# TensorE's expert jobs written out, and the last job's rows added to the tokens by gate matrices on chip

## The chip, the cores and the metric

The kernel runs on one core of a Trainium2 chip. Its time is device time in microseconds from a run's start to its end; lower is better. In the trace, PE is TensorE's matmul side and PEld its weight loads, DVE is VectorE, ACT is ScalarE, POOL is GpSimd, and SP is the engine whose queue issues most DMAs.

## The reference

Two layers of a hybrid backbone over 256 latent tokens of width 1024 with 256 context tokens. The change lies in the channel mixer of the second layer, a top-2-of-8 expert SwiGLU in float32, and in the norm and residual behind it:

```python
logits = (xt @ w_router) + b_router
top_v, top_e = lax.top_k(logits, TOP_K)            # TOP_K = 2, N_EXPERTS = 8
gates = jax.nn.softmax(top_v, axis=-1)
...
def expert_block(args):
    xblk, e = args
    g, u = jnp.split(xblk @ w_gu[e], 2, axis=-1)   # 1024 -> 2 x 3584
    return (jax.nn.silu(g) * u) @ w_dn[e]          # 3584 -> 1024
yb = yb * row_gate[:, None]
... .at[row_tok].add(yb)                           # each token: the sum of its two gated rows
x = x + gt2 * rmsnorm(channel_mixer(hx, ...), g_post_ffn[l])
```

The kernel returns the latent stream after both layers.

## The kernel before

Everything up to the router (both mixers, the dense feed-forward network of layer 0) is untouched by the change and ends at about 1,376 us of the span. What follows is the expert stage.

**Jobs.** The 512 token-expert pairs are sorted by expert and cut into jobs of at most `CAP` = 96 rows of one expert. DVE works out on chip the list of jobs, their number, and for each token the two rows that it holds in that list (`rt[:, 0:4]`, and as whole numbers `posi`) with the two gates (`rt[:, 4:8]`). With the inputs given there are 8 jobs, one for each expert. POOL scatters the token rows to DRAM (`moe_rows`), from where SP fetches the 96 rows of a job.

**A job on PE.** A job's weights are 42 slabs of 1 MB: 28 for gate and up (seven groups `q` of four), 14 for down. SP brings them into a ring of 14 slab buffers; it issues a slab when PE has released the buffer (`e_used`), and PE waits for it by `e_raw`. Each slab is 24 float32 matmuls of 256 columns, which go to four column groups of the array (`products`, L1691; the trace shows each as two records, so 48 records a slab). After the first slab of each group PE transposes the group before (`transposes`, three, L1701), between DVE's product and copy; after the seventh down slab it transposes the next job's rows (eight, L1723). On PE, ACT and DVE the job is the body of a loop (`Fori(0, n_jobs)`) whose count is read from `jobs` at run time; SP has job 0 written out and a loop over the rest.

**Order around a job's end.** ACT takes silu of each group's gate half (L892, L894), copies the next job's rows out of PSUM (L885), then the result `O` to `yb` (L898, L899), and sends it to DRAM (`moe_out`) by four DMAs (L902), whose landings count in `y_out`. `yb` holds 96 rows in an odd form: partition 32c + r and index g are row 32g + r and columns 256c to 256c + 255.

**After the last job.** ACT waits for all landings (L905), loads a table and signals POOL, which fetches each token's two rows of `moe_out` by four indirect DMAs (L605, `back`). ACT multiplies the first by its gate (L909), DVE adds the gated second (L1344), ACT squares and sums (L912) and takes the root (L914), DVE forms a diagonal of reciprocals (L1347, L1348), PE multiplies tokens by it, which also turns them (L1732), DVE adds them to the stream `xm` (L1351), and SP writes it out (L555).

Of the kernel before, what the change touches and what calls it, by code (L numbers as in the profile page):

```python
# [28 lines left out]
P = 128  # L29
D = 1024  # L30
# [28 lines left out]
N_LIST = MAX_JOBS + 1  # L59

# [92 lines left out]
def build_program(nc, a, out):  # L153
    ctx = ExitStack()
    with ctx:
# [73 lines left out]
        back = [[view(M, 8192 + 2048 * c + D * n, D) for n in range(2)] for c in range(2)]  # L229
        part1 = [view(M, 12288 + D * n, D) for n in range(2)]  # L230
# [62 lines left out]
        f_part, f_tok, f_sq, f_sd, f_diag, f_t = (sem(n) for n in ("f_part", "f_tok", "f_sq", "f_sd", "f_diag", "f_t"))  # L293
# [185 lines left out]
        def _(sp):  # L479
# [53 lines left out]
            n_jobs = sp.value_load(jobs[0:1, N_LIST:N_LIST + 1], min_val=1, max_val=MAX_JOBS)  # L533
# [10 lines left out]
            with sp.Fori(1, n_jobs) as j:  # L544
                e = sp.value_load(jobs[0:1, bass.ds(j, 1)], min_val=0, max_val=NE - 1)
                for i in range(JOB_SLABS):
                    sp.wait_ge(e_used, j * JOB_SLABS + (i + 1))
                    expert_slab(e, i, i)
                    if i == 12:
                        sp.wait_ge(e_gath, j + 1)  # L550
                        rows_of(j + 1)

# [60 lines left out]
        def _(act):  # L613
# [265 lines left out]
            n_jobs = act.value_load(jobs[0:1, N_LIST:N_LIST + 1], min_val=1, max_val=MAX_JOBS)  # L879
# [9 lines left out]
            with act.Fori(0, n_jobs) as j:  # L889
                for q in range(GU_GROUPS):  # L890
                    act.wait_ge(e_used, j * JOB_SLABS + (RAW_E + 4 * q + 4))
                    act.activation(tge[:, q % 2, 0:2, :], S[q % 2][:, :].rearrange("p (a b) -> p a b", b=256)[:, :, 0:P],  # L892
                                   ACT.Silu).then_inc(e_silu, 1)
                    act.activation(tge[:, q % 2, 2, :], T[q % 2][:, 0:P], ACT.Silu).then_inc(e_silu, 1)  # L894
                take_rows(j + 1)
                act.wait_ge(e_used, j * JOB_SLABS + (RAW_E + JOB_SLABS))
                act.wait_ge(y_out, j * 64 + 64)
                act.activation(yb[:, 0:2, :], O[0][:, :].rearrange("p (a b) -> p a b", b=256), ACT.Copy).then_inc(e_yb, 1)  # L898
                act.activation(yb[:, 2, :], O[1][:, 0:256], ACT.Copy).then_inc(e_yb, 1)  # L899
                act.wait_ge(e_yb, j * 2 + 4)  # L900
                for c in range(4):
                    act.dma_start(ys[bass.ds(j, 1), :, :, 256 * c:256 * c + 256].rearrange("a g p n -> (a p) g n"),  # L902
                                  yb[32 * c:32 * c + 32, :, :]).then_inc(y_out, 16)

            act.wait_ge(y_out, n_jobs * 64 + 64)  # L905
            act.activation(tab[:], eps[0:1, :], ACT.Sqrt).then_inc(ys_ready, 1)
            for n in range(2):
                act.wait_ge(rows_back[0][n], 16)
                act.activation(part1[n], back[0][n], ACT.Copy, scale=rt[:, 4 + n:5 + n]).then_inc(f_part, 1)  # L909
            for n in range(2):  # L910
                act.wait_ge(f_tok, n + 1)
                act.activation(part1[n], ytok[n], ACT.Square, accum_out=rt[:, 176 + n:177 + n]).then_inc(f_sq, 1)  # L912
                act.wait_ge(f_sq, n + 1)
                act.activation(rt[:, 178 + n:179 + n], rt[:, 176 + n:177 + n], ACT.Sqrt, scale=1.0 / D, bias=eps[:]).then_inc(f_sd, 1)  # L914
# [5 lines left out]
        def _(dve):  # L920
# [390 lines left out]
            own.link(dve.tensor_copy(jobs[0:1, N_LIST:N_LIST + 1], end[0:1, 7:8]))  # L1311
            dve.wait_ge(ht_copied, 4)
            own.link(dve.memset(rt[0:1, 160:161], 0.0))
            dve.memset(rt[0:1, 163:164], 0.0).then_inc(y_out, 64)
# [3 lines left out]
            n_jobs = dve.value_load(jobs[0:1, N_LIST:N_LIST + 1], min_val=1, max_val=MAX_JOBS)  # L1318
# [6 lines left out]
            with dve.Fori(0, n_jobs) as j:  # L1325
# [23 lines left out]
            for k in range(KT):  # L1349
                dve.wait_ge(f_t, k // 2 + 1)  # L1350
                dve.scalar_tensor_tensor(xm[:, 0, k, :], [S[0], S[1], T[0], T[1]][k // 2][:, SEQ * (k % 2):SEQ * (k % 2) + SEQ],  # L1351
# [6 lines left out]
        def _(pe):  # L1358
# [19 lines left out]
            def keep_up(n):  # L1378

                for _ in range(n):  # L1380
                    mm(T[1][:, 0:P], mean[:], mean[:], start=True, stop=True)
# [292 lines left out]
            n_jobs = pe.value_load(jobs[0:1, N_LIST:N_LIST + 1], min_val=1, max_val=MAX_JOBS)  # L1674
# [9 lines left out]
            with pe.Fori(0, n_jobs) as j:  # L1684
# [20 lines left out]
                for q in range(GU_GROUPS):  # L1705
                    if q >= 2:
                        pe.wait_ge(e_h, j * 2 * GU_GROUPS + (2 * q - 2))
                    for s in range(4):
                        products(4 * q + s, lambda k, g: xg[:, 2 * s + k, 32 * g:32 * g + 32], (S[q % 2], T[q % 2]), s == 0, s == 3)
                        if s == 0 and q:  # L1710
                            transposes(q - 1)
                pe.wait_ge(e_yb, j * 2 + 2)
                for d in range(DN_SLABS):
# [5 lines left out]
                    if d == 6:  # L1719
# [6 lines left out]

            for n in range(2):
                pe.wait_ge(f_diag, n + 1)
            for k in range(KT):
                for n in range(2):  # L1730
                    c = SEQ * (k % 2) + P * n
                    ins = mm([S[0], S[1], T[0], T[1]][k // 2][:, c:c + P], ytok[n][:, P * k:P * k + P], diag[:, n, :],  # L1732
# [164 lines left out]
```

## Time and profile before

| | us |
|---|---|
| median of 3 runs | 2393.02 (2390.64 to 2393.62) |
| the profiled execution, its own time | 2392.59 |
| its span, first to last instruction | 2390.8 |
| PE busy | 2274.5 (95%) |
| DVE / ACT / POOL busy | 752.7 / 572.0 / 48.5 |
| expert stage on PE, first to last slab matmul | 1397.17 to 2363.14 |
| from there to the span's end | 27.7 |

PE's busy share hides what matters here: a pause of 5 to 6 us between two jobs is 4% of a job. The span is read in three parts: up to 1,397 us (layers before the expert jobs), the eight jobs, and the end. Only the last two are touched, save for a few small instructions of the router. A pause of PE shows in the timeline as an idle time in square brackets with what ended it; "issue" there means that no semaphore seen by the profile did. PEclk in a table of stretches is the granted clock of TensorE, 1.00 being 2.4 GHz and 0.50 being 1.2 GHz.

### The profile page before, as it was taken

How to read it: one execution, taken by the hardware profiler on the slowest of the kernel's cores; microseconds unless marked ns; L12 is line 12 of the kernel's file. 1: busy time of each engine (PE TensorE's matmuls, PEld its weight loads, DVE VectorE, ACT ScalarE, POOL GpSimd, SP SyncE). 2: the span in 40 equal slices, each digit the busy share in tenths (PEclk: the TensorE clock that was granted, in tenths of full speed). 3: DMA queues.
4: the chain of work that ended last, by engine and by line, in shares of the span. 5: the costliest groups of instructions: out<-in, count | busy, mean ns of one | idle time of the engine just before them, and what ended most of it. 6: DMA issues, size and time to landing. Idle time of an engine off the chain costs nothing.

```text
span 2390.8 us, 55761 instructions
## 1 busy us (share of the span) xinstructions
PE 2274.5 (95%) x24654; PEld 1644.5 (69%) x24654; DVE 752.7 (31%) x1513; ACT 572.0 (24%) x1094; POOL 48.5 (2%) x63
## 2 busy tenths in 40 slices
PE   7999999999999999989999999899999999999996
PEld 4777877777777887768989875555555555555554
DVE  4465345445532233477377610000101010101011
ACT  4245334323322222245355410000000000000001
POOL 0000010000200000000010000000000000000000
PEclk8999999999999999999999999999999999999998
DMA  6323232324843343212234869999999999999991
GB/s 248 116 107 141 82 130 97 133 106 159 284 176 118 127 176 131 97 65 96 105 137 146 315 265 393 361 376 356 385 365 379 362 379 362 378 358 386 361 377 63
DMA packets 86755, 549.92 MB, mean 230 GB/s; under 512 B 10336, under 2 KB 13920, under 8 KB 26496
## 3 DMA queue, kind: packets, MB, share of 16 engines
q1 hardware_dynamic: 76176, 521.91, 57.3%
q0 software_dynamic: 4176, 14.81, 1.9%
q10 hardware_dynamic: 6176, 9.70, 1.3%
q8 instruction: 200, 3.28, 0.5%
q14 instruction: 27, 0.22, 0.0%
HBM read 529.47 MB, written 16.91 MB: 229 GB/s over the span
## 4 chain that ended last, share of the span: by engine, by line
PE 44%; issue 43%; DVE 8%; ACT 2%; DMA 1%; POOL 0%; ACTq 0%; POOLq 0%; SPq 0%; DVEq 0%
PE pp L1363 9%; PE pp L1365 8%; PE pp L1364 8%; PE S L1363 2%; DVE wsp L926 2%; PE S L1364 2%; PE S L1365 2%; PE T L1365 2%; PE T L1363 2%; PE T L1364 2%; PE pp L1398 1%; PE T L1494 1%; ACT wsp L622 1%; PE O L1481 1%; PE S L1461 1%
## 5 line engine op out<-in xcount | busy, mean ns | idle before, releaser
L1691 PE MATMUL S<-slabs,M 128*32 128x256 f32 x7168 | 480.7, 387 | 37.3 <-issue 37.3
L1691 PEld LDWEIGHTS S<-slabs,M 128*32 128x32 f32 x7168 | 229.1, 112 | 201.2 <-issue 59.3
L926 DVE TENSOR_TENSOR wsp<-raw,wsp 128x1024 fp32r<-128x1024 f32 (+3 forms) x248 | 264.0, 1086 | 323.8 <-ACT wsp L622 322.6
L1363 PE MATMUL pp<-hx,wsp 128*128 128x512 f32 (+1 forms) x800 | 285.0, 356 | 19.8 <-DVE M L1137 4.7
L1333 DVE TENSOR_TENSOR M<-M,S 128x256 f32<-128x256 f32 x56 | 23.6, 421 | 865.2 <-ACT M L892 865.2
L1691 PE MATMUL O<-slabs,M 128*32 128x256 f32 x5376 | 294.9, 379 | 0.0
L1691 PE MATMUL T<-slabs,M 128*32 128x256 f32 x3584 | 279.8, 385 | 0.0
L1365 PE MATMUL pp<-hx,wsp 128*128 128x512 f32 (+1 forms) x800 | 277.4, 347 | 0.0
L1364 PE MATMUL pp<-hx,wsp 128*128 128x512 f32 (+1 forms) x800 | 277.4, 347 | 0.0
L1691 PEld LDWEIGHTS O<-slabs,M 128*32 128x32 f32 x5376 | 173.1, 110 | 114.9 <-issue 1.3
L622 ACT ACTIVATE wsp<-raw 128x1024 fp32r<-128x1024 f32 (+3 forms) x248 | 224.2, 935 | 28.8 <-PE pp L1365 19.9
L1363 PEld LDWEIGHTS pp<-hx,wsp 128*128 128x128 f32 x800 | 154.5, 193 | 49.4 <-DVE M L1172 7.0
L1363 PE MATMUL pp<-opr,wsp 128*128 128x512 f32 (+1 forms) x496 | 177.8, 359 | 2.8 <-DVE opr L1179 1.5
L1364 PE MATMUL pp<-opr,wsp 128*128 128x512 f32 (+1 forms) x496 | 176.0, 355 | 0.0
L1365 PE MATMUL pp<-opr,wsp 128*128 128x512 f32 (+1 forms) x496 | 176.0, 355 | 0.0
L1691 PEld LDWEIGHTS T<-slabs,M 128*32 128x32 f32 x3584 | 117.2, 112 | 80.9 <-issue 5.0
L1365 PEld LDWEIGHTS pp<-hx,wsp 128*128 128x128 f32 x800 | 154.2, 193 | 18.6
L1364 PEld LDWEIGHTS pp<-hx,wsp 128*128 128x128 f32 x800 | 154.6, 193 | 16.2
L892 ACT ACTIVATE M<-S 128x256 f32<-128x256 f32 x56 | 21.5, 384 | 598.1 <-PE T L1691 598.1
L1363 PEld LDWEIGHTS pp<-opr,wsp 128*128 128x128 f32 x496 | 93.7, 189 | 17.8 <-DVE opr L1179 2.2
L1365 PEld LDWEIGHTS pp<-opr,wsp 128*128 128x128 f32 x496 | 93.7, 189 | 13.2
L1364 PEld LDWEIGHTS pp<-opr,wsp 128*128 128x128 f32 x496 | 93.8, 189 | 12.8
(215 smaller groups left out, 2342.5 us busy)
## 6 DMA issues: line engine op xcount, KB each, us to landing
slabs<-in_w_moe SPq DMA_DIRECT2D x336, 1024.0 KB, 7.2
raw<-in_w_main SPq DMA_DIRECT2D x84, 1024.0 KB, 4.9
M<-in_w_main SPq DMA_DIRECT2D x40, 1024.0 KB, 5.0
raw<-in_w_br SPq DMA_DIRECT2D x24, 512.0 KB, 3.6
xm<-in_w_main SPq DMA_DIRECT2D x8, 1024.0 KB, 5.0
raw<-in_w_dn SPq DMA_DIRECT2D x8, 768.0 KB, 4.2
moe_rows<-M POOLq DMA_DIRECT2D x14, 384.0 KB, 9.6
raw<-in_w_dn SPq DMA_DIRECT2D x8, 640.0 KB, 3.9
```

Of the source, the lines that this page charges most:

```text
L622: act.activation(wsp[:, slot, 0, 0:w], raw[:, rslot, half * w:half * w + w], ACT.Copy).then_inc(hi_done, 1)
L892: act.activation(tge[:, q % 2, 0:2, :], S[q % 2][:, :].rearrange("p (a b) -> p a b", b=256)[:, :, 0:P], ACT.Silu).then_inc(e_silu, 1)
L926: dve.tensor_tensor(wsp[:, slot, 1, 0:w], raw[:, rslot, half * w:half * w + w], wsp[:, slot, 0, 0:w], ALU.subtract).then_inc(lo_done, 1)
L1333: dve.tensor_tensor(hse[:, q % 2, 0:2, :], tge[:, q % 2, 0:2, :], S[q % 2][:, :].rearrange("p (a b) -> p a b", b=256)[:, :, P:256], ALU.mu ...
L1363: mm(dst, w_hi, x_hi, start=first, stop=False)
L1364: mm(dst, w_hi, x_lo, start=False, stop=False)
L1365: return mm(dst, w_lo, x_hi, start=False, stop=last)
L1398: ins = mm(dst[r0:r0 + 32, 0:256], c32[:, k, :], w[:, 256 * k:256 * k + 256], start=(k < 4), stop=(k >= 4))
L1461: ins = mm(S[half][:, N * c:N * c + N], q[h, :], keys[h, k0 + N * c:k0 + N * c + N], start=True, stop=True)
L1481: ins = mm(O[ot % 2][HD * half:HD * half + HD, P * qt:P * qt + P], V[:, k, vc:vc + HD], prT[:, half, n, :], start=(n == 0), stop=(n == len ...
L1494: ins = pe.transpose(T[half][:, P * k:P * k + P], pr[:, half, P * k:P * k + P], ident[:])
L1691: ins = mm(banks[g // 2][32 * c:32 * c + 32, 256 * (g % 2):256 * (g % 2) + 256], x(k, g), slab_e[i % RAW_E][:, 1024 * k + 256 * c:1024 * k ...
```

## The change

**PE's jobs.** The loop body becomes a function `job(j, first, more)`. At least eight jobs run now (`MIN_JOBS` = 8; surplus jobs would work on empty rows). Jobs 0 to 5 are written out one after the other; a loop runs from job 6 up to `last`, the index of the last job (7 here, so it runs once); the last job is written out behind it, without the transposes of a next job's rows. ACT has job 0 written out, a loop over jobs 1 to 6, and the last apart; DVE has a loop over jobs 0 to 6 and the last apart; SP has job 0, a loop over 1 to 6, and the last, which fetches no rows.

**Gate matrices.** After the one-hots of job 0, DVE builds for all 256 tokens the 96 columns of the last job: the token's gate where it has that row, else zero (`og_tok`, 12 products of 128x128 and an addition, in the free buffer `raw`). During job 0 PE turns them by two sets of three transposes (in the third slab of groups 3 and 5), and ACT copies them to `og`.

**The other jobs' rows.** After job 6 ACT waits until its result is in DRAM, then signals POOL, which fetches all tokens' rows during the last job; a row of the last job reads as the zeros that `moe_out` was filled with. DVE, after its own work for the last job, sums them with the gates (`early`, four instructions of 1024 columns).

**The end.** The last result does not go to DRAM. ACT and DVE copy it to `yb` side by side; PE multiplies it by the gate matrices, 24 matmuls with 32 rows of contraction, 128 columns of weights and 256 moving columns, going round the four row groups and into four PSUM banks for each half of the tokens; DVE adds `early` in eight pieces; ACT squares in four halves of 512 columns; DVE adds the two partial sums; the rest is as before, with 14 small matmuls (`keep_up`) ahead of the diagonal ones.

The diff, cut to its core:

```diff
@@ SP
-            with sp.Fori(1, n_jobs) as j:
+            def job(j, more):
...
+            with sp.Fori(1, last) as j:
+                job(j, True)
+            job(last, False)
@@ ACT
-            with act.Fori(0, n_jobs) as j:
+            def channels(j, first=False):
...
+                    if first and q in (3, 5):
+                        n = (q - 3) // 2
+                        act.wait_ge(og_T, n + 1)
+                        act.activation(og[:, :, P * n:P * n + P], pp[1][:, 0:TG * P].rearrange("p (a b) -> p a b", b=P),
+                                       ACT.Copy).then_inc(og_copied, 1)
...
-            act.wait_ge(y_out, n_jobs * 64 + 64)
-            act.activation(tab[:], eps[0:1, :], ACT.Sqrt).then_inc(ys_ready, 1)
+            job(0, True)
+            with act.Fori(1, last) as j:
+                job(j)
+
+            act.wait_ge(y_out, last * 64 + 64)
+            act.activation(tab[:], eps[0:1, :], ACT.Copy).then_inc(ys_ready, 1)
+            channels(last)
+            act.activation(tab[:], eps[0:1, :], ACT.Sqrt)
+            act.wait_ge(e_used, last * JOB_SLABS + (RAW_E + JOB_SLABS))
+            act.activation(yb[:, 0:2, :], O[0][:, :].rearrange("p (a b) -> p a b", b=256), ACT.Copy).then_inc(e_yb, 1)
             for n in range(2):
-                act.wait_ge(rows_back[0][n], 16)
-                act.activation(part1[n], back[0][n], ACT.Copy, scale=rt[:, 4 + n:5 + n]).then_inc(f_part, 1)
+                for h in range(2):
+                    act.wait_ge(f_tok, 4 * n + 2 * h + 2)
+                    act.activation(back[n][h][:, 0:512], ytok[n][:, 512 * h:512 * h + 512], ACT.Square,
+                                   accum_out=rt[:, 200 + 2 * n + h:201 + 2 * n + h]).then_inc(f_sq, 1)
@@ DVE
+            own.link(dve.tensor_scalar(rt[:, 182:183], end[:, 7:8], float(MIN_JOBS), -float(CAP), ALU.max, ALU.mult))
...
+                        own.link(dve.tensor_scalar(og_tok[c][:, n, g, :].rearrange("p (a b) -> p a b", b=32), slot,
+                                                   rt[:, 188 + 4 * g + 2 * c + n:189 + 4 * g + 2 * c + n],
+                                                   rt[:, 4 + 2 * c + n:5 + 2 * c + n], ALU.is_equal, ALU.mult))
+            dve.tensor_tensor(og_tok[0], og_tok[0], og_tok[1], ALU.add).then_inc(og_ready, 1)
...
+            with dve.Fori(0, last) as j:
+                job(j)
+            job(last)
             for n in range(2):
-                dve.wait_ge(f_part, n + 1)
+                dve.wait_ge(rows_back[0][n], 16)
                 dve.wait_ge(rows_back[1][n], 16)
-                dve.scalar_tensor_tensor(ytok[n], back[1][n], rt[:, 6 + n:7 + n], part1[n], ALU.mult, ALU.add).then_inc(f_tok, 1)
+                own.link(dve.tensor_scalar(early[n], back[0][n], rt[:, 4 + n:5 + n], None, ALU.mult))
+                own.link(dve.scalar_tensor_tensor(early[n], back[1][n], rt[:, 6 + n:7 + n], early[n], ALU.mult, ALU.add))
+            dve.wait_ge(e_used, last * JOB_SLABS + (RAW_E + JOB_SLABS))
+            dve.tensor_copy(yb[:, 2, :], O[1][:, 0:256]).then_inc(e_yb, 1)
+            for n in range(2):
+                for c in range(4):
+                    dve.wait_ge(f_y, 4 * n + c + 1)
+                    dve.tensor_tensor(ytok[n][:, 256 * c:256 * c + 256], y_bank[n][c][:, 0:256], early[n][:, 256 * c:256 * c + 256],
+                                      ALU.add).then_inc(f_tok, 1)
@@ PE
-            with pe.Fori(0, n_jobs) as j:
+            def job(j, first=False, more=True):
...
+                        if first and s == 2 and q in (3, 5):
...
+                            for g in range(TG):
+                                ins = pe.transpose(pp[1][:, P * g:P * g + P], og_tok[0][:, n, g, :], ident[:])
+                            ins.then_inc(og_T, 1)
...
+            for j in range(MIN_JOBS - 2):
+                job(j, first=(j == 0))
+            with pe.Fori(MIN_JOBS - 2, last) as j:
+                job(j)
+            job(last, more=False)
+
+            pe.wait_ge(e_yb, last * 2 + 4)
+            for n in range(2):
+                for g in range(TG):
+                    for c in range(4):
+                        lanes = slice(32 * c, 32 * c + 32)
+                        ins = mm(y_bank[n][c][:, 0:256], og[lanes, g, P * n:P * n + P], yb[lanes, g, :], start=(g == 0), stop=(g == TG - 1))
+                        if g == TG - 1:
+                            ins.then_inc(f_y, 1)
+            pe.wait_ge(f_tok, 1)
+            keep_up(14, S[0])
```

What this moves, on PE at the boundary of two jobs. Before, the end of the loop body and what is behind the loop (`O` and `S` are the banks of down and of gate and up; L1732 are the diagonal matmuls of the end):

```order
L1723 MATMUL pp<-ident,M 128x96 x8
L1691 MATMUL O<-slabs,M 32x256 x168
L1684 REGISTER_ALU
L1684 COMPARE_AND_BRANCH
L1732 MATMUL S<-M 128x128 x8
L1732 MATMUL T<-M 128x128 x8
L155 UNCONDITIONAL_BRANCH
```

Of the changed kernel, the boundary of jobs 0 and 1, both written out:

```order
L1788 MATMUL pp<-ident,M 128x96 x8
L1746 MATMUL O<-slabs,M 32x256 x168
L1746 MATMUL S<-slabs,M 32x256 x8
L1746 MATMUL T<-slabs,M 32x256 x4
```

The jump back to the body's first instruction is gone; the next job's first slab stands right behind the last one of the job before.

The end of PE's program in the changed kernel (L1803 are the gate-matrix matmuls, L1435 is `keep_up`, L1813 the diagonal ones):

```order
L1746 MATMUL O<-slabs,M 32x256 x48
L1798 REGISTER_ALU
L1803 MATMUL S<-M 128x256 x2
L1803 MATMUL T<-M 128x256 x2
...
L1803 MATMUL pp<-M 128x256 x2
L1803 MATMUL O<-M 128x256 x2
L1435 MATMUL S<-mean 128x128 x14
L1813 MATMUL S<-M 128x128 x8
L1813 MATMUL T<-M 128x128 x8
```

Between the last slab and the diagonal matmuls, where nothing stood before, there are now 24 gate-matrix matmuls and 14 of `keep_up`.

On ACT, what stands between the sending of a result and the first silu of the job behind it. Before, the silu is preceded by a load of its table in every turn of the loop:

```order
L889 UNCONDITIONAL_BRANCH
L889 ISA
L892 ACT_TABLE_LOAD
L892 ACTIVATE M<-S 128x256
L894 ACTIVATE M<-T 128x128
```

In the changed kernel, from job 6 to the last (L926 is the wait for the landing of job 6's result):

```order
L919 DMA moe_out<-M 32x3x256
L923 REGISTER_ALU
L923 COMPARE_AND_BRANCH
L926 ISA
L927 ACTIVATE tab<-eps 1x1
L900 ISA
L901 ACTIVATE M<-S 128x256
L903 ACTIVATE M<-T 128x128
```

The wait for the result's landing now stands ahead of the last job's first silu, and no table load does.

## Rows read from the trace of the kernel before

**Rows 1.** Chain that ended last, from 2,362 us on: start, us, what

```profile
1392.11 975.84 issue
...
2371.97 5.94 DMA M<-moe_out,posi
```

**Rows 2.** Waits in the expert stage: engine, line, releaser, us, times, longest

```profile
PE S L1691 <- issue: 37.3, 7, 6.0
...
SPq L522 <- PE T L1691: 548.3, 224, 11.7
```

**Rows 3.** Timeline of PE: start, us, line, operation, count, [idle before <-releaser]

```profile
1397.17 1.07 PE L1691 MATMUL S<-slabs,M 128*32 128x256 f32 x16
...
1499.80 11.62 PE L1691 MATMUL O<-slabs,M 128*32 128x256 f32 x212
1517.40 1.93 PE L1691 MATMUL S<-slabs,M 128*32 128x256 f32 x16 [5.98 <-issue]
...
1532.74 1.07 PE L1691 MATMUL S<-slabs,M 128*32 128x256 f32 x16
...
1534.06 1.05 PE L1691 MATMUL S<-slabs,M 128*32 128x256 f32 x16
...
1536.65 1.05 PE L1691 MATMUL S<-slabs,M 128*32 128x256 f32 x16
...
1543.71 1.07 PE L1691 MATMUL S<-slabs,M 128*32 128x256 f32 x16
...
1614.27 0.88 PE L1723 MATMUL pp<-ident,M 96*128 96x96 f32 x8
1615.08 18.34 PE L1691 MATMUL O<-slabs,M 128*32 128x256 f32 x336
1638.67 1.93 PE L1691 MATMUL S<-slabs,M 128*32 128x256 f32 x16 [5.26 <-issue]
```

**Rows 4.** Stretches: length, busy (x) of PE, PEld, DVE, ACT, POOL, PEclk, DMA share, GB/s

```profile
1511.50:1517.40 5.90, 0.00 (x0) 0.01 (x1) 0.00 (x0) 2.15 (x3) 0.00 (x0) 0.73 1.02 336
1517.40:1521.40 4.00, 4.00 (x44) 1.99 (x48) 0.00 (x0) 0.00 (x0) 0.00 (x0) 0.54 0.80 276
1525.00:1633.00 108.00, 108.00 (x1937) 63.71 (x1933) 7.69 (x21) 4.74 (x16) 0.00 (x0) 1.00 0.99 382
```

**Rows 5.** DMA queues, 1511.5 to 1517.4 us: packets, MB, share

```profile
q8 instruction: 2, 0.03, 2.2%
```

**Rows 6.** DMA issues, 1438 to 1460 us, then 1485 to 1508: count, KB, us to landing

```profile
slabs<-in_w_moe SPq DMA_DIRECT2D x8, 1024.0 KB, 9.9
...
slabs<-in_w_moe SPq DMA_DIRECT2D x9, 1024.0 KB, 7.2
```

**Rows 7.** Timeline of ACT and DVE inside jobs, and the landings of L902's DMAs

```profile
1408.23 0.42 DVE L1333 TENSOR_TENSOR M<-M,S 128x256 f32<-128x256 f32 x1 [18.23 <-ACT M L892]
...
1512.61 1.82 ACTq L902 DMA_DIRECT2D moe_out<-M  x4
...
DMA to landing us min/median/max: 1.9/7.8/9.2
```

**Rows 8.** Timeline of a score group: two row groups of 64, weights of 128 columns

```profile
1125.95 1.13 PE L1461 MATMUL S<-M 64*128 64x256 f32 x8
```

**Rows 9.** Timeline of the end, all engines

```profile
2363.29 0.60 ACT L898 ACTIVATE M<-O 128x512 f32<-128x512 f32 x1 [17.50 <-PE O L1691]
...
2378.02 1.28 DVE L1344 SCALAR_TENSOR_TENSOR M<-M 128x1024 f32<-128x1024 f32 x1 [1.89 <-DMA M<-moe_out,posi]
...
2379.34 1.06 ACT L912 ACTIVATE M<-M 128x1024 f32<-128x1024 f32 x1
...
2381.47 3.52 PE L1732 MATMUL S<-M 128*128 128x128 f32 x16 [18.33 <-DVE M L1348]
2384.84 1.95 PE L1732 MATMUL T<-M 128*128 128x128 f32 x16
...
2385.93 1.77 DVE L1351 SCALAR_TENSOR_TENSOR xm<-T,am,xm 128x256 f32<-128x256 f32 x4
```

More of the change, by code:

```diff
@@ L228, in build_program @@
         zero = view(M, 5120, D)
-        back = [[view(M, 8192 + 2048 * c + D * n, D) for n in range(2)] for c in range(2)]
-        part1 = [view(M, 12288 + D * n, D) for n in range(2)]
+        back = [[raw[:, c, D * n:D * n + D] for n in range(2)] for c in range(2)]
+        early = [view(M, 12288 + D * n, D) for n in range(2)]
+        og_tok = [raw[:, c, 0:2 * TG * P].rearrange("p (a b c) -> p a b c", b=TG, c=P) for c in range(2)]
+        og = view(M, 1024, TG, SEQ)
         ytok = [view(M, 2048 + D * n, D) for n in range(2)]
@@ L532, in _ @@
             sp.wait_ge(routed, 1)
-            n_jobs = sp.value_load(jobs[0:1, N_LIST:N_LIST + 1], min_val=1, max_val=MAX_JOBS)
+            last = sp.value_load(jobs[0:1, N_LIST + 1:N_LIST + 2], min_val=MIN_JOBS - 1, max_val=MAX_JOBS - 1)
             def rows_of(j):
@@ L878, in _ @@
             act.wait_ge(routed, 1)
-            n_jobs = act.value_load(jobs[0:1, N_LIST:N_LIST + 1], min_val=1, max_val=MAX_JOBS)
+            last = act.value_load(jobs[0:1, N_LIST + 1:N_LIST + 2], min_val=MIN_JOBS - 1, max_val=MAX_JOBS - 1)
             def take_rows(j):
@@ L1317, in _ @@
             dve.wait_ge(routed, 1)
-            n_jobs = dve.value_load(jobs[0:1, N_LIST:N_LIST + 1], min_val=1, max_val=MAX_JOBS)
+            last = dve.value_load(jobs[0:1, N_LIST + 1:N_LIST + 2], min_val=MIN_JOBS - 1, max_val=MAX_JOBS - 1)
             for n in range(2):
@@ L1323, in _, with job @@
             dve.tensor_tensor(oh, oh, oh2, ALU.add).then_inc(e_onehot, 1)
-            with dve.Fori(0, n_jobs) as j:
+            own.link(dve.tensor_scalar(rt[:, 182:183], end[:, 7:8], float(MIN_JOBS), -float(CAP), ALU.max, ALU.mult))
+            own.link(dve.tensor_scalar(rt[:, 184:188], rt[:, 0:4], rt[:, 182:183], float(CAP), ALU.add, ALU.add))
+            for g in range(TG):
+                own.link(dve.tensor_scalar(rt[:, 188 + 4 * g:192 + 4 * g], rt[:, 184:188], -32.0 * g, None, ALU.add))
+            slot = iota[:, 0:32].rearrange("p (a c) -> p a c", a=1).to_broadcast([P, 4, 32])
+            for n in range(2):
+                for c in range(2):
+                    for g in range(TG):
[3 more added lines that the diff above has]
+            dve.tensor_tensor(og_tok[0], og_tok[0], og_tok[1], ALU.add).then_inc(og_ready, 1)
+            def job(j):
                 def keep(q):
@@ L1718, in _ @@
                         transposes(GU_GROUPS - 1)
-                    if d == 6:
+                    if d == 6 and more:
+                        if first:
+                            pe.wait_ge(og_copied, 2)
                         pe.wait_ge(e_hT, j * GU_GROUPS + GU_GROUPS)
```

39 lines of the change are left out of this document (27 added, 12 removed).

## The prediction

> **What bounds the kernel now.** I read the chain of waits first. It ends in the fetch of the tokens' rows and before that shows one piece of 975.84 us called issue [rows 1]: the eight jobs, for which the chain names no releaser. So I went to the waits of that stage. SP, which issues the weight slabs, waits for PE 548.3 us in 224 places at gate-and-up slabs alone [rows 2]. The ring is therefore full, and PE, not the DMA queue, sets the pace. PE itself is idle seven times, 37.3 us in all [rows 2], once between each two jobs.
>
> The timeline of PE shows what a boundary is [rows 3]. Job 0 runs from 1397.17 to 1511.42 (the row of 1499.80 plus its 11.62), 114.25 us without a gap. Then PE pauses 5.98 us; job 1 runs 1517.40 to 1633.42, 116.0 us for the same work, and a pause of 5.26 us follows. Two costs, then. The first is the pause. No semaphore ended it, and in it the DMA table shows two packets of the instruction queue [rows 5], while slabs issued before had landed: I read it as the fetch of the loop body's first instructions after the jump back. The second is the clock: the granted clock is 1.00 through the 108 us of a job's middle, falls in the pause (0.73 on average) and is 0.54, nearly the 1.2 GHz level, in the 4 us after it [rows 4]. That is where the 1.8 to 2.8 us come from by which later jobs are longer than job 0. The stage takes 2363.14 - 1397.17 = 965.97 us; eight jobs like job 0, end to end, would take 8 x 113.93 + 0.33 = 911.8 (a matmul record lasts 0.38 us but the next starts 0.05 after it, so 0.33 of the 114.25 overlap the next job).
>
> After the last job PE stands still for 18.33 us until the diagonal matrices are there [rows 9]: copies, a trip to DRAM and back, two gated sums, squares.
>
> **Part 1, the jump back.** In the new order the first slab of jobs 1 to 6 stands right behind its forerunner. Job 6 is a loop body run once, job 7 is behind the loop. Entering a loop has no price: job 0's first row in the trace of before has no idle time ahead of it [rows 3], and it too was the entry of this loop. Leaving it without a jump back lets instructions run on in a straight line, as within the 114 us of a job. What else could hold the next job is early: its rows are copied during the down slabs, its slabs are in the ring. So all seven pauses go: 965.97 - 911.8 = 54.2 us gained. Bounds: nothing below, since job 0 has no pause; above, one or two pauses with their slow clock stay, for the loop around job 6, at 54.2 / 7 = 7.7 us each.
>
> The rows speak for a fetch; the Trainium skill (Runtime: NRT & Kernel Launch, Instruction fetch mechanics) says the same of a taken branch whose target lies outside the pages held, and that fetching in a straight line is mostly hidden. By it the pauses go as well.
>
> **Part 2, small work on PE in the jobs.** Two sets of three transposes come into job 0. One set costs 0.62: four slabs with one set take 1543.71 - 1532.74 = 10.97, and four slabs without are 4 x 2.59 = 10.36 (1534.06 to 1536.65) [rows 3]. Together +1.2. The last job drops eight transposes: -0.8 (1614.27 to 1615.08). In the router one more linked DVE instruction stands ahead of `routed`: +0.2. The gate matrices themselves are some 18 small DVE instructions, at 0.42 each [rows 7] under 8 us, in the 18.23 us in which DVE was idle before its first product of job 0 [rows 7]; nobody waits. The sum is +0.6; were that cover gone, DVE would be late by those 8 us in job 0.
>
> **Part 3, the wait added on ACT.** ACT now waits for the landing of job 6's result before the last job's first silu; behind it queue all silus of that group, DVE's product, and PE's transposes after the fifth slab. ACT sends from 1512.61 for 1.82 us, and a landing takes 7.8 in the median and 9.2 at most [rows 7], so in terms of the job's start the wait ends at 1.2 + 1.8 + 7.8 = 10.8 to 12.2. The fifth slab ends at 5 x 2.59 = 12.95, and silus and products need about 1.1 (two of each, pipelined, 0.42 the longest). PE thus waits between nothing and 0.4 if the landings are as before; I take 0.3, and up to 3 in the range, since the result now travels beside slabs that never pause. A signal given late costs POOL nothing: its fetches have 100 us.
>
> **Part 4, DMA.** The 2 MB of fetched rows now travel beside the last job's slabs. At 382 GB/s [rows 4] they are 5.5 us of transfer. The ring's lead is 14 x 2.6 = 36 us less a landing of 7.2 to 9.9 [rows 6], so nothing is late. The other question is whether slabs keep up without the pauses. In job 0 the time to landing was 9.9 at 1438 to 1460 us and fell to 7.2 at 1485 to 1508 while PE ran without a pause [rows 6]: the transfers caught up against PE's full pace. Cost zero.
>
> **Part 5, the end.** From the last slab's end (T):
> - T + 0.8: both copies to `yb` (ACT's starts at 0.15 and takes 0.60 [rows 9]) and the semaphore; DVE's shorter one runs beside it.
> - Gate-matrix matmuls. The trace has no four row groups. The nearest is a score group with two: 8 records, 4 matmuls of 256 columns, in 1.13 [rows 8], less the 0.38 of the last record 0.107 for each record. At that pace 48 records take 5.1; if four groups run abreast as two did, half, 2.6. I take 2.6, since in the score group pairs are in step and a float32 matmul of 256 columns in four column groups shows that pace (2.59 for 48 records of a slab [rows 3]). The first half's banks are then ready at 1.5.
> - DVE's eight additions of 256 columns at 0.42 [rows 7]: they start at 1.5 and end at 1.5 + 3.4 = 4.9. With the slow pace they would end at about 5.9 and `keep_up` (14 x 0.25, the pace of two records of L1732 at full clock, 1.95 for 16) would become the last: +1.9 in all.
> - From the last addition to the diagonal matmuls before: 2381.47 - 2379.30 = 2.17 [rows 9]. Half a square instead of a whole one gives back 0.4, the addition of two sums costs 0.25: 2.0.
> Together T + 7.7, against T + 18.33 before: 10.6 gained, 8.7 with the slow pace. The multiplication by the first gate, the sum with the second and the root's table load now lie under the last job's down slabs (DVE about 5 us of 36).
>
> The diagonal matmuls run at full clock instead of starting at half: 3.8 us for 32 records at 0.112 (L1732's second row) against 3.52 + 1.95; DVE ends 0.9 behind them, and the way out is unchanged at 3.1. So 7.8 from their start to the end, against 9.33: 1.5 gained.
>
> The skill (TensorE: Matmul & The Clock Gate, Part 3: Packing small matmuls) gives 3.07 times for four row tiles at 512 columns; by that 24 matmuls of 0.43 take 3.4, and the sum would end 0.3 later. No row here shows four row groups.
>
> **The sum.** 1397.17 + 0.2 + 911.8 + (1.2 - 0.8 + 0.3) = 2309.9 for the last slab; + 7.7 = 2317.6; + 7.8 = 2325.4 of span. The profiled execution took 1.8 more than its span (2392.59 against 2390.8), so **2327.2 us**. Its own time stood 0.4 below the median of the runs, less than the runs differ among themselves.
>
> **Rivals.**
> - *The slabs fall behind.* For it speaks a DMA share of 0.99 inside jobs [rows 4], and that each pause lets the queue catch up. If 382 GB/s were all there is, a job's 45.1 MB (42 slabs, its rows in and out, its instructions) would take 118.1 us; 4.2 x 8 = 33.6 late, of which the ring's lead of about 30 swallows all but some 4: 2331. At 370 GB/s it would be 121.9 a job and 2361. Against it stands the falling time to landing. Between 2331 and 2361, chance 0.06.
> - *A pause or two stay* at the loop kept around job 6: 2327 + 7.7 or + 15.4, so 2335 to 2343, chance 0.05.
> - *The pauses are not the jump's* and stay at all seven places. Only the end gains: 2392.6 - 12.1 + 1 = 2381.5. Against it: seven of seven stand at the jump, none elsewhere. Chance 0.02.
> - *Slower: the clock.* Without rests the granted clock is lowered during the eight jobs. A job at a share s of the clock takes 113.9 / s; with the end's gain the kernel is slower than before once 8 x (113.9 / s - 113.9) passes 65 us, at s under 0.933. A third of the stage at the half level would cost 300 us: 2630. Against it: 1.00 over 108 us and half clock only behind pauses [rows 4]. Chance 0.03.
> - The forecast itself 0.84.
>
> **How the numbers follow.** The forecast's own bounds are 2324 (DVE's additions overlap, no stall on ACT) and 2332 (slow pace of the gate-matrix matmuls, 3 us on ACT). The range goes on into the first two rivals: 2323.5 to 2336. What remains outside is the rest of those and the last two. A measurement of this kernel tells 0.2%, some 5 us, from no change. Faster by more than that: forecast and first three rivals, 0.97, of which 0.01 goes to a mixture that ends within 0.2%; within: 0.01; slower: 0.03.
>
> **What would show it.** Right: no idle time of PE at the seven boundaries, job starts 114 us apart, granted clock 1.00 from 1,400 us to the end; last slab at about 2,310; gate-matrix matmuls in 2.6 to 5.1 us; diagonal matmuls some 7.7 after the last slab. Wrong: SP's waits for PE shrinking and slabs landing more than 20 us after issue (first rival); instruction packets with a gap at job 6 or 7 (second); stalls of PE after the last job's fifth slab over 3 us (part 3); a clock under 1.00 amid a job (fourth).

## The result and the profile after

The changed kernel takes **2331.1 us** (median of 4 runs, 2329.7 to 2332.8) against 2392.9 in the same comparison: a ratio of 0.974 (95% interval 0.973 to 0.976). The forecast was 2327.2 with a range of 2323.5 to 2336.0. Medians of one kernel differ by a few us from one comparison to another: in those further down the changed kernel has 2334.0 once, and the kernel before 2390.6 to 2394.0. The profiled execution took 2331.1 us with a span of 2329.3, so the span came out 3.9 us above the 2325.4 of the sum.

The page of the changed kernel: span, PE, and the chain that ended last, by engine. Before, the chain named PE for 44% and "issue" (time in which the profile shows nothing that was waited for) for 43%; now that PE runs from job to job it can be followed through the expert stage.

```profile
span 2329.3 us, 55813 instructions
PE 2265.9 (97%) x24728; PEld 1648.0 (71%) x24728; DVE 763.8 (33%) x1545; ACT 560.3 (24%) x1089; POOL 48.6 (2%) x63
PE 85%; DVE 9%; ACT 3%; issue 2%; DMA 1%; ACTq 0%; DVEq 0%; SPq 0%
```

The timeline of PE at the boundary of jobs 0 and 1 (start, us, line, operation, count), to be held against the 5.98 us of idle time in [rows 3]:

```profile
1508.73 3.85 PE L1746 MATMUL O<-slabs,M 128*32 128x256 f32 x68
1512.40 1.05 PE L1746 MATMUL S<-slabs,M 128*32 128x256 f32 x16
```

No idle time stands in brackets behind these rows, and the 16 records of the first slab take 1.05 us where they took 1.93 behind a pause. The waits of the expert stage (engine, what, releaser, us in total, times, longest) answer [rows 2]:

```profile
ACT tab L927 <- DMA moe_out<-M: 13.3, 1, 13.3
PE pp L1756 <- DVE M L1375: 2.5, 1, 2.5
```

The seven waits for "issue" of 37.3 us are gone, and PE has a new one of 2.5 us. Stretches (length, busy of PE, PEld, DVE, ACT, POOL, PEclk, DMA share, GB/s): jobs 0 to 6 and the first 12 us of the last, then the 4 us behind the new wait.

```profile
1397.00:2209.00 812.00, 812.00 (x14551) 481.05 (x14553) 53.89 (x147) 40.61 (x129) 0.00 (x0) 1.00 1.00 391
2212.50:2216.50 4.00, 3.96 (x47) 2.17 (x51) 0.00 (x0) 0.00 (x0) 3.09 (x4) 0.68 1.00 421
```

For 812 us on end PE is busy at the full level of the clock. The place of the new wait, on ACT, DVE and PE (job 6's last slab ends at 2197.1, the last job's fifth at 2210.0):

```profile
2211.36 0.20 ACT L927 ACTIVATE tab<-eps 1x1 f32<-1x1 f32 x1 [13.29 <-DMA moe_out<-M]
2211.47 0.36 ACT L901 ACTIVATE M<-S 128x256 f32<-128x256 f32 x1
2211.73 0.27 ACT L903 ACTIVATE M<-T 128x128 f32<-128x128 f32 x1
...
2211.86 0.42 DVE L1372 TENSOR_TENSOR M<-M,S 128x256 f32<-128x256 f32 x1 [48.98 <-ACT M L901]
2212.20 0.28 DVE L1375 TENSOR_TENSOR M<-M,T 128x128 f32<-128x128 f32 x1
2212.54 0.55 PE L1756 MATMUL pp<-ident,M 128*128 128x128 f32 x3 [2.54 <-DVE M L1375]
```

Read backwards: PE waits for DVE's product, DVE for ACT's silu, ACT for the landing of job 6's result. And the end, answering [rows 9]:

```profile
2314.50 0.60 ACT L931 ACTIVATE M<-O 128x512 f32<-128x512 f32 x1 [34.81 <-PE O L1746]
2314.50 0.42 DVE L1389 COPY M<-O 128x256 f32<-128x256 f32 x1 [29.19 <-PE O L1746]
2315.15 0.48 PE L1803 MATMUL S<-M 32*128 32x256 f32 x2 [0.72 <-ACT M L931]
...
2316.74 0.76 DVE L1393 TENSOR_TENSOR M<-S,M 128x256 f32<-128x256 f32 x2 [1.82 <-PE T L1803]
...
2317.64 0.38 PE L1803 MATMUL O<-M 32*128 32x256 f32 x2
...
2318.74 0.75 DVE L1393 TENSOR_TENSOR M<-O,M 128x256 f32<-128x256 f32 x2
...
2321.49 2.02 PE L1813 MATMUL S<-M 128*128 128x128 f32 x16
2323.35 1.95 PE L1813 MATMUL T<-M 128*128 128x128 f32 x16
```

The last slab ends at 2314.43, the gate-matrix matmuls run from 2315.15 to 2318.02, and the diagonal ones start 7.06 us after the last slab, where it was 18.33.

### The profile page after: what moved, and what is told of

It is laid out like the page before. It is cut to its first block, busy times and chain, and to the rows that moved or that the text cites. A ratio compares the mean times of both kernels' runs of the same rounds, so it can differ in the third digit from the quotient of the medians.

```text
span 2329.3 us, 55813 instructions
## 1 busy us (share of the span) xinstructions
PE 2265.9 (97%) x24728; PEld 1648.0 (71%) x24728; DVE 763.8 (33%) x1545; ACT 560.3 (24%) x1089; POOL 48.6 (2%) x63
## 4 chain that ended last, share of the span: by engine, by line
PE 85%; DVE 9%; ACT 3%; issue 2%; DMA 1%; ACTq 0%; DVEq 0%; SPq 0%
PE S L1746 17%; PE O L1746 13%; PE pp L1417 9%; PE pp L1419 8%; PE pp L1418 8%; PE T L1746 8%; PE S L1417 2%; DVE wsp L951 2%; PE S L1418 2%; PE S L1419 2%; PE T L1418 2%; PE T L1417 2%; PE T L1419 2%; PE pp L1452 1%; PE T L1548 1%
## 5 line engine op out<-in xcount | busy, mean ns | idle before, releaser
L1746 PE MATMUL S<-slabs,M 128*32 128x256 f32 x7168 | 471.5, 380 | 0.0
```

The costliest lines, as they stand in the source:

```text
L1746: ins = mm(banks[g // 2][32 * c:32 * c + 32, 256 * (g % 2):256 * (g % 2) + 256], x(k, g), slab_e[i % RAW_E][:, 1024 * k + 256 * c:1024 * k ...
```

## The experiments

Three theories were to be told apart: where the gain came from (the jumps back, or the end), what a jump back costs and why, and where the 4 us are that the sum missed. Each kernel below was compared with the kernel before, on one chip for each group of kernels: `e2` to `e5` (before: 2390.6 us), `e1` and `e6` to `e8` (2393.2), `e9` (2391.5), `e10` to `e12` (2394.0).

### Each half of the change alone

`e2_only_written_out` is the kernel before with this edit:

```diff
-            with pe.Fori(0, n_jobs) as j:
+            def job(j):
...
+            for j in range(7):
+                job(j)
+            with pe.Fori(7, n_jobs) as j:
+                job(j)
```

> The kernel before, with PE's jobs 0 to 6 written out and a loop run once for job 7; nothing else changed (the end stays as it was). Theory (the pauses between jobs and the slow clock behind them come from PE's jump back to the start of a long loop body): all seven go, 54.2 us less, so 2338.7, and no idle time of PE between jobs. The landing of the results' DMAs should rise from a median of 7.8 us to about 10.6, as in the changed kernel, since the slabs no longer pause; here nobody waits for them early. Rival (the pauses come from something else at a job's end, or the end gave most of the gain): 2381 to 2393.

Measured: 2339.1 us (2336.7 to 2339.7), ratio 0.978 (0.977 to 0.980). PE's stage, first to last slab matmul, is 912.5 us long (it was 965.97) with no idle time, and its only wait is the one at the end, 17.9 us. The landings of the results' DMAs (minimum, median, maximum):

```profile
DMA to landing us min/median/max: 1.9/10.7/14.7
```

The median was 7.8 [rows 7]: with PE never pausing, results land 3 us later, though nothing about their sending was changed. The two kernels that follow bear this out: with five jumps back left the median is 7.9, with two it is 9.6.

`e3_only_end` is the changed kernel with jobs 1 to 6 in a loop again:

```diff
-            for j in range(MIN_JOBS - 2):
-                job(j, first=(j == 0))
-            with pe.Fori(MIN_JOBS - 2, last) as j:
+            job(0, first=True)
+            with pe.Fori(1, last) as j:
                 job(j)
```

> The changed kernel with jobs 1 to 6 of PE as the body of a loop again (jobs 0 and 7 written out, so five jumps back); its end as changed. Theory: five pauses of 5 to 6 us, each followed by a slow clock, 5 x 7.7 = 38.7 more than the changed kernel: 2369.8. At the boundaries of jobs 0 and 1 and of jobs 6 and 7, which have no jump back, no pause. Rival (a loop's entry and exit cost as much as a jump back): seven pauses, 2385.

Measured: 2369.9 us (2369.1 to 2370.1), ratio 0.991 (0.990 to 0.993). The waits of PE:

```profile
PE S L1746 <- issue: 26.0, 5, 5.7
PE pp L1756 <- DVE M L1375: 3.1, 1, 3.1
```

Five pauses for five jumps back; none where job 0 enters the loop and none where the loop is left for job 7. So an entry and an exit are free, and a jump back costs (2369.9 - 2331.1) / 5 = 7.8 us, of which 5.2 is pause and the rest the slow clock behind it. The two medians are from two comparisons, and the lengths of PE's stage in the two profiles say 8.1: (957.9 - 917.3) / 5, with a wait on DVE that was 0.6 us longer in this kernel.

### Is it the jump or the body?

`e4_two_a_turn` puts two jobs in a turn:

```diff
-            with pe.Fori(1, last) as j:
-                job(j)
+            with pe.Fori(0, 3) as t:
+                for half in range(2):
+                    job(t * 2 + (1 + half))
```

> As only_end, but the loop body holds two jobs and turns three times (jobs 1 to 6), so two jumps back. Theory (a price for each jump back, whatever the body's length): 2 x 7.7 = 15.4 more than the changed kernel, 2346.5, pauses only at the boundaries of jobs 2 and 3 and of jobs 4 and 5. Rival (a price for each instruction of the body, all fetched again): the same total as with one job a turn, 2370.

Measured: 2345.6 us (2344.3 to 2347.2), ratio 0.981 (0.980 to 0.983), 14.5 us above the changed kernel. In the timeline of PE the two jumps back stand where two turns meet:

```profile
1745.19 1.93 PE L1746 MATMUL S<-slabs,M 128*32 128x256 f32 x16 [5.80 <-issue]
...
1980.02 1.93 PE L1746 MATMUL S<-slabs,M 128*32 128x256 f32 x16 [5.20 <-issue]
```

The price is 7.2 us for a jump by the medians, and 8.3 by the stage, which is 933.8 us long and holds a wait on DVE of 3.5 us instead of 2.5. So it is about the same whether one job or two lie between jumps; 0.6 us more or less for a jump is not resolved here. The rival, a price for each instruction fetched again, is out.

`e5_quiet_queue` is `e3_only_end` with the slabs of jobs 1 to 7 cut to 16 of 2048 columns; the rest of the weights that it multiplies are leftovers. The core of the edit:

```diff
-                sp.dma_start(slab_e[i % RAW_E], a["w_moe"][bass.ds(e * JOB_SLABS + r, 1), :, :]
+                w = 2048 if small is None else 16
+                sp.dma_start(slab_e[i % RAW_E][:, 0:w], a["w_moe"][bass.ds(e * JOB_SLABS + r, 1), :, 0:w]
```

> As only_end (five jumps back), but of the weight slabs of jobs 1 to 7 only 16 of the 2048 columns are fetched, so that the DMA engines are nearly idle when PE jumps (the weights multiplied are then leftovers). Theory (the pause is the wait for two packets of instructions that share the DMA engines with the slabs): the pause shrinks from 5.0 to 6.0 us to about 3, two packets of about 1 us and what lies around them, and with it the slow clock may go. Rival (a fixed time of the sequencer): 5.0 to 6.0 us as before.

Measured: 2351.6 us (one run). The waits of PE, and the stretches of 4 us after the first jump back, of this kernel and then of `e3_only_end` (columns as above):

```profile
PE S L1747 <- issue: 17.0, 5, 3.8
PE T L1747 <- issue: 1.1, 2, 0.8
```

```profile
1624.70:1628.70 4.00, 4.00 (x52) 2.30 (x56) 0.00 (x0) 0.00 (x0) 0.00 (x0) 0.65 0.34 80
```

```profile
1630.20:1634.20 4.00, 4.00 (x40) 1.99 (x44) 0.00 (x0) 0.00 (x0) 0.00 (x0) 0.50 0.94 310
```

The pause shrinks from 5.2 to 3.4 us in the mean (2.4 to 3.8), where about 3 was expected, so part of it is the traffic of the slabs, and the larger part is there with a nearly idle queue too. The clock still falls, but later: 0.8 to 1.3 us after PE has resumed, where in `e3_only_end` it had fallen within each of the five pauses. (The waits of T are not at a jump; more on them below.)

The traces say more on what the pause is. Here is the instruction queue (packets, MB, share) in 0.2 us of the first pause of the kernel before, 1514.50 to 1514.70, and of the second pause of this kernel, 1741.40 to 1741.60, with the row of PE behind the latter:

```profile
q8 instruction: 1, 0.02, 34.0%
```

```profile
q8 instruction: 1, 0.02, 33.2%
1744.16 1.07 PE L1747 MATMUL S<-slabs,M 128*32 128x256 f32 x16 [3.58 <-issue]
```

In both, PE resumes 2.7 to 2.8 us after this packet, the last one ahead of its first matmul. The same holds behind all 19 jumps back of the four kernels (7, 5, 2 and 5): 2.6 to 2.9 us from the start of the last packet to PE's first matmul, and once 3.2. Beside the slabs this packet starts 2.2 to 3.2 us after PE has stopped; in the quiet kernel it starts between 0.2 us before the stop and 1.1 after it. So the pause ends at nearly the same distance, some 2.7 us, behind a fetch of instructions, with traffic or without, and what the slabs lengthen is the time until the last packet starts. Of the two theories, the first had the shorter pause right and the clock wrong; a fixed time, the second, fits only these last 2.7 us.

### The four us that were missing

`e1_wait_later` moves the wait for the landing, and the signal to POOL with it, behind two of the last job's seven groups:

```diff
-            act.wait_ge(y_out, last * 64 + 64)
-            act.activation(tab[:], eps[0:1, :], ACT.Copy).then_inc(ys_ready, 1)
-            channels(last)
+            channels(last, range(2))
+            act.wait_ge(y_out, last * 64 + 64)
+            act.activation(tab[:], eps[0:1, :], ACT.Copy).then_inc(ys_ready, 1)
+            channels(last, range(2, GU_GROUPS))
```

> The changed kernel, with ACT's wait for the landing of job 6's result (and the signal to POOL) moved behind the silus of the first two groups of the last job. Theory (the sum came out 4 us low because ACT waited 13.3 us for that landing, which held PE 2.54 us ahead of the last job's first transposes and cost another 1.7 by the slow clock behind it): 4.2 us less than the changed kernel, 2326.9, no idle time of PE between 1,397 us and the last slab. Rival (the missing 4 us lie elsewhere, as in slabs that land late): 2331.

Measured: 2327.1 us (2325.1 to 2330.8), ratio 0.973 (0.971 to 0.974). The wait of 2.5 us is gone. The stage takes 914.7 us against 917.3. But 4.2 less than 917.3, so 913.1, was expected, and the profile has one odd place:

```profile
2225.02 0.47 PE L1747 MATMUL S<-slabs,M 128*32 128x256 f32 x4 [0.77 <-issue]
```

From 2222.3 to here PE's matmuls came thinly, 2.9 us after the first of POOL's four fetches had started (2219.36). Three kernels on one chip tell chance from cause: this one again, one with the wait behind five groups (`range(5)` in both places of the edit above), and the changed kernel again, without an edit.

> As wait_later, with ACT's wait and the signal to POOL moved behind the silus of the fifth group of the last job, some 33 us later. In the profile of wait_later PE's matmuls came thinly for 2.7 us (2222.3 to 2225.0) just after POOL's four fetches went out. Theory (a chance late packet of instructions, unrelated to the fetches): 2327 as wait_later. Rival (the fetches hold up what feeds PE): the same thin stretch some 33 us later, about 2327, and with fetches hidden either way no time between the two.

> The changed kernel itself, on the same chip as the two with a later wait, for a direct comparison: 4 us above them, 2331.

> The kernel of wait_later once more, on the same chip as the changed kernel: 2327, 4 us below it. If the thin stretch of matmuls behind POOL's fetches is no chance, its profile shows it again at about 2222 us; the profile without it should have a span of about 2325.

Measured, in this order: 2325.9 us (2325.1 to 2328.6), ratio 0.972 (0.970 to 0.973); 2334.0 (2329.7 to 2335.7), ratio 0.974 (0.973 to 0.976); 2325.8 (2324.2 to 2328.1), ratio 0.971 (0.970 to 0.973). The two kernels with a later wait came out 1 us under what was expected, and the changed kernel 3 us over it. The stages of the three profiles last 913.0, 920.0 and 912.8 us, and neither the first nor the last has a thin stretch or an idle time of PE before the last slab. Of the timeline of `e12_wait_later_again`, around the last job's first transposes and the wait, now behind the second group:

```profile
2209.09 0.27 ACT L903 ACTIVATE M<-T 128x128 f32<-128x128 f32 x1
...
2211.27 0.55 PE L1757 MATMUL pp<-ident,M 128*128 128x128 f32 x3
...
2220.23 0.18 ACT L928 ACTIVATE tab<-eps 1x1 f32<-1x1 f32 x1
2220.68 0.99 POOL L614 DMA_INDIRECT raw<-moe_out,posi  x1 [828.89 <-ACT tab L928]
```

The silus are 2.2 us ahead of the transposes, and when ACT comes to the wait it has no idle time: the result has long landed. The thin stretch of `e1_wait_later` is not there again, so it doesn't belong to the place of the wait. But it is not unique: the waits of T in `e5_quiet_queue` are such a stretch, 3.1 us behind the start of its first fetch. Two profiles show it and `e10` and `e12`, with the same fetches, don't; whether the fetches have a part in it stays open.

What the wait costs is 917.3 - 912.8 = 4.5 us of the stage in the first profile and 920.0 - 912.8 = 7.2 in the one on this chip. A row of the latter shows where most of the difference comes from:

```profile
2215.83 0.90 PE L1756 MATMUL pp<-ident,M 128*128 128x128 f32 x3 [3.38 <-DVE M L1375]
```

The pause is 0.8 us longer than the 2.54 of the first profile, and PE starts at the lower level of the clock, with 0.90 for three transposes that took 0.55 there, and stays at it until 2222.0: about 3.1 us lost in work at half pace, against 1.7 in the first profile. That leaves some 0.6 unexplained. The pause is 2.5 to 3.5 us in all eight profiles that have this wait, and the changed kernel's 2.54 is the shortest. By the medians the later wait is worth 4.1 us (across two comparisons) and 8.2 (within one). It is the fastest version: 2325.8 to 2327.1.

### Pieces of the end

`e6_row_groups_in_turn` swaps the two inner loops of the gate-matrix matmuls:

```diff
-                for g in range(TG):
-                    for c in range(4):
+                for c in range(4):
+                    for g in range(TG):
```

> The changed kernel with the 24 gate-matrix matmuls in another order: three in a row go to the same row group and bank (c outer, g inner). Theory (row groups work abreast only if neighbours differ): each half then takes 12 x 0.43 = 5.1 us, less what overlaps where the group changes, the phase 8 to 10 us instead of 2.86, and the end 5 to 7 us later. Rival (the phase is bound by its weight loads of 128 columns, in any order): 2.9 as now.

Measured: 2333.4 us (one run). Its timeline, first and last row of the phase and what follows:

```profile
2315.32 1.45 PE L1803 MATMUL S<-M 32*128 32x256 f32 x8 [0.72 <-ACT M L931]
...
2320.60 3.39 PE L1435 MATMUL S<-mean 128*128 128x128 f32 x28
...
2323.83 1.39 PE L1813 MATMUL S<-M 128*128 128x128 f32 x11
```

The phase takes 5.28 us up to the first of `keep_up`, against 2.80 (2315.15 to 2317.95) in the changed kernel. The order matters, but less than expected, 5.3 us instead of 8 to 10: 48 records at 0.11 each, where by an estimate one row group by itself would take 0.22 for a record (one of 128 columns takes 0.112 in the row of L1732 in [rows 9], second bank, and these have 256). This is the slow pace that the prediction had as its upper bound. Why it isn't slower still, the two rows don't say; between them the timeline has rows of two banks interleaved, so neighbouring groups seem to overlap there. In this order three matmuls in a row also go to the same PSUM bank, and no run separates the bank from the row group. `keep_up` becomes the last thing ahead of the diagonal matmuls, as was said; they start 9.2 us after the last slab instead of 7.06.

`e7_no_keep_up` leaves the line `keep_up(14, S[0])` out.

> The changed kernel without the 14 small matmuls ahead of the diagonal ones. PE is then idle for some 3.5 us. Theory (they hold the clock up): the diagonal matmuls start at the half level, the first 16 records take about 3.5 instead of 2.02 us, and the span's end is 1 to 1.5 us later. Rival (3.5 us of idle time do not lower the clock, or DVE behind them sets the end): no difference of the end.

Measured: 2331.6 us (one run), but its last slab ended 1.17 us earlier than in the changed kernel (2313.26), so the end is 16.44 us long against 14.87: 1.6 us longer. A row of the timeline of PE, and the stretches from its start (columns as above):

```profile
2320.31 2.59 PE L1812 MATMUL S<-M 128*128 128x128 f32 x16 [3.46 <-DVE M L1402]
```

```profile
2320.30:2321.40 1.10, 1.09 (x10) 1.10 (x11) 0.00 (x0) 0.00 (x0) 0.00 (x0) 1.00 0.00 0
2321.40:2325.40 4.00, 4.00 (x24) 4.00 (x23) 2.50 (x6) 0.00 (x0) 0.00 (x0) 0.57 0.18 73
```

After 3.46 us of idle time the first sixteen records take 2.59 us, between the 1.95 of full clock and the 3.52 of [rows 9], and the stretches show why: the granted clock is 1.00 when they start and then 0.57 in the mean, near the lower level: it fell some 1.3 us after PE had resumed.

`e8_fetch_twice` sends POOL's four fetches twice, the second time each behind its first landing, and DVE waits for both:

```diff
-            for n in range(2):
+            for n in range(4):
+                twice, n = n > 1, n % 2
                 for c in range(2):
+                    if twice:
+                        pool.wait_ge(rows_back[c][n], 16)
```

> The changed kernel with the 2 MB of tokens' rows fetched twice during the last job, each second fetch behind the landing of its first. Theory (the fetch is hidden and the slabs have 28 us of lead): no difference, 2331, PE without an idle time after the one at the last job's start. Rival (the fetch already costs something beside the slabs): some us more.

Measured: 2330.4 us (one run), no more than the changed kernel. PE's only wait before the last slab is the one on DVE, 3.2 us. 2 MB more beside the slabs cost nothing that this run resolves.

`e9_half_matmuls` cuts the loop over the two halves of a slab to one:

```diff
-                    for k in range(2):
+                    for k in range(1):
```

> The changed kernel with half of each slab's matmuls left out (the second 128 of 256 rows of contraction), so that PE needs 1.3 us for a slab and the DMA queue must set the pace: it shows how much the slabs could be supplied at. The time of a job divides its 45 MB. If the supply is what first-rival thinking feared, 382 GB/s, a job takes 118 us and longer than with all matmuls; if it is about 415 to 425 GB/s, as seen in short stretches, a job takes 106 to 109 us, and the changed kernel at 391 GB/s runs at 92 to 94% of it. Total then 8 x (113.9 - 107) = 55 us less than the changed kernel, less the ring's lead: about 2300 or lower.

Measured: 2268.2 us (one run). The stretch from 1,500 to 2,150 us, the DMA issues in it (count, KB, us to landing), and PE's wait for slabs of gate and up from 1,397 to 2,250 us:

```profile
1500.00:2150.00 650.00, 407.77 (x6106) 203.81 (x6099) 44.48 (x121) 32.55 (x104) 0.00 (x0) 0.98 1.01 410
```

```profile
slabs<-in_w_moe SPq DMA_DIRECT2D x249, 1024.0 KB, 28.0
```

```profile
PE S L1746 <- DMA slabs<-in_w_moe: 195.0, 187, 2.7
```

Now the queue sets the pace, at 410 GB/s (415 to 425 was expected, and some 2276 us), and a slab lands 28 us after its issue. In the same stretch the changed kernel draws 396, and a slab lands after 8.1. The DMA share reads 1.01 in the one and 1.00 in the other: it does not tell a queue that keeps up from one that holds PE back. The time to landing does.

## Why the prediction was right, and what it missed

**Part 1, the jump back: right.** Seven pauses gone, the clock at 1.00 between, 54.2 us forecast; the kernel with this part alone is 53.9 us faster than the first median shown of before (2393.0) and 51.5 faster than the median of its own comparison (2390.6), and its stage fell from 965.97 to 912.53, 53.4 us. The reading of the pause as a fetch after a jump is borne out: the number of pauses follows the jumps (7, 5, 2, 0), entries and exits are free, and each of 19 pauses ends some 2.7 us behind the start of an instruction packet. The price for each, 7.7, was measured as 7.8 and 7.2 by the medians. This is also what the Trainium skill says (Runtime: NRT & Kernel Launch, Instruction fetch mechanics), that a taken branch out of the pages held waits for a DMA fetch; the trace agrees, with two packets of the instruction queue in a pause of 5.98 us [rows 5], and adds the clock behind it, about a third of the price. The rival of a pause or two that stay fell. One reading was a little off, and nothing rested on it: later jobs are 1.4 to 2.9 us longer than job 0, not 1.8 to 2.8.

**Part 3, the wait on ACT: the step that was mis-sized.** It named the right wait, the right queue behind it and the right place, PE's transposes after the fifth slab, and put 0.3 us on it with 3 as the worst. It cost 2.54 us of pause and nearly 2 more, 4.5 in all (7.2 in the second profile of this kernel), 4.2 more than forecast. With 0.6 more elsewhere in the stage, 0.2 less ahead of it and 0.6 less at the end that is the distance of 3.9 between the sum and the span. Two errors. The wait ended 14.5 us after the job's start (2211.36 against 2196.86), where the text had 10.8 to 12.2; the 1.1 for silus and products was right (1.2). The landing was taken as 7.8 to 9.2 from a trace in which the jumps' pauses gave the queue a rest just when results left; without them it is 10.6 in the median and 14.8 at most, as the kernel with part 1 alone shows by itself (10.7 and 14.7). The text said that results would travel beside slabs that never pause, and did not take the value from that. And PE's pause was priced without the slow clock behind it, though the same text had just read that cost behind the other pauses. The 4.5 passes the 3 that the text had as the worst. That the result still lies within the forecast's own bounds, 2324 to 2332, is in part luck: the upper one also holds 1.9 us for a slow pace of the gate matrices that did not come.

**Part 4, DMA: right**, and the rival of slabs that fall behind fell, with its headroom now known: 396 GB/s used of 410. The slabs issued from 2200 to 2215 us, when the fetches went out, took 9.6 us to land in the median, of a lead of 36. The argument from falling landing times was sound; the argument from the share of 0.99 would have misled.

**Part 5, the end: right within 0.6 us.** The diagonal matmuls start 7.06 us after the last slab (7.7 forecast): the row groups ran abreast at nearly the pace chosen (2.87 us for 2.6), and DVE's first addition starts at T + 2.3 as forecast (0.8 + 1.5). The 0.6 comes from the additions, which overlap: all eight take 2.75 us instead of 3.4. The Trainium skill's 3.07 times (TensorE: Matmul & The Clock Gate, Part 3) would have given 3.4 us by the prediction's estimate. The trace shows 2.87 us, which is 3.6 times against the 10.3 (24 x 0.43, an estimate) of matmuls one after the other. From there to the end it is 7.8 us as forecast. `keep_up` is worth 1.6 us, close to the 1.5 that the forecast had for diagonal matmuls that start at the full level.

**Part 2** cannot be told from the rest by more than a few tenths. The stage without the wait takes 912.8 us where the sum had 912.2 (911.8 + 1.2 - 0.8), which leaves 0.6 for it and all else.

**The rival on the slower side**, a clock lowered in eight jobs without a rest, did not come: 1.00 over 812 us.

## What to carry to other kernels

In this kernel a loop body of some 2,000 TensorE matmul records costs a pause at each jump back, though no data is waited for: 5.2 us, and half as much again for the clock. Writing the jobs out or putting more work in a turn removes it in proportion to the jumps. Look for it as an idle time "issue" at the first instruction of a loop body. When a change removes a pause, re-measure every landing time that was taken from beside it, since a queue that had rests in the old trace will have none in the new; and put a wait for such a landing behind work that doesn't need it. To see how near a full queue is to holding the engine back, look at time to landing, or halve the engine's work once; its busy share was 1.00 and 1.01 here.

## What the runs showed of the hardware that I had not expected

The pause after a jump back is 3.4 us long even with the DMA engines nearly idle (5.2 beside slabs), so quiet traffic alone does not make such a loop cheap; PE resumes some 2.7 us after the start of the last instruction packet in both. A small write of 96 KB beside a queue that draws 391 GB/s takes 10.6 us to land where it took 7.8 with short rests, though a 1 MB read beside it takes 7.9. Three matmuls in a row to one row group of 32, and to one bank, reach half the pace of four groups in turn (5.28 against 2.80 us for 24).

And how long TensorE has been idle does not tell by itself at which level of its clock it starts again. After 3.46 us (`e7`), after 2.54 (the changed kernel) and after up to 3.84 (`e5`) it started at the full level and fell to the lower one 0.8 to 1.4 us into the work; after 3.13 (`e3`) and 3.38 (`e11`) it started at the lower level. Even the pause of 2.54 us was followed by the lower level, so a pause of this length is not free of that cost.
